# Banded heads among half output tiles, weights ahead of x, gate slabs in the first cross attention, a third MLA weight buffer

## The chip, the cores and the metric

The kernel runs on one core of a Trainium2 chip. The metric is the time of one execution on the device in microseconds; of several runs the median is taken. TensorE multiplies matrices into PSUM, VectorE and ScalarE work element by element and also read PSUM, GpSimd is a slower vector engine, SyncE (SP) mostly starts DMA transfers. Each engine runs its own instructions in order, and engines wait for one another by semaphores.

## What is computed

A model of two blocks over 512 tokens of width 1024, with a memory of 256 tokens, in float32. Cut to what matters:

```
x = x + pool_conv_mixer(rmsnorm(x))              # layer 0; layer 1: x + mla_attention(rmsnorm(x)), 16 heads
x = x + cross_attention(rmsnorm(x), rmsnorm(mem))  # 4 heads of 256; k, v = mem @ wkv; each layer
x = x + conv_ffn(rmsnorm(x))                     # up 1024 -> 2 x 2816, taps, silu, down; each layer
x = rmsnorm(x)                                   # then the second block, one layer:
shift, scale, gate = split(silu(c) @ w_ada + b_ada)
h = rmsnorm(x) * (1 + scale) + shift
sb_q, sb_k, sb_v, sb_g, sw_q, sw_k, sw_v, sw_g = split(h @ w_in)
y_sb = stick_breaking(sb_q, sb_k, sb_v) * silu(sb_g)            # 8 heads of 64
y_sw = window_attention(sw_q, sw_k, sw_v, sinks) * silu(sw_g)   # 8 heads, band of 128 keys and a sink
x = x + gate * (concat(y_sb, y_sw) @ w_out)
return rmsnorm(x)
```

## The kernel before

x lives transposed in SBUF, as 8 tiles of 128 channels by 512 tokens. A weight matrix passes as slabs of 128x2048 elements (1 MB), usually all 1024 input rows by 256 columns. Products are made in three: each slab and each input is split into a high part (ScalarE's copy to fp32r, `w_hi`, `h_hi`) and a low part (VectorE's difference, `w_lo`, `h_lo`), and for each 128x128 piece TensorE does hi*hi, hi*lo and lo*hi. An output tile is 128 channels by 512 tokens, 24 matmuls over 8 pieces, in one PSUM bank; a slab gives two tiles. `ORDER` lists all slabs. `LOADS` is the order in which SP starts their transfers. Split slabs go through two raw buffers and two pairs of `w_hi`, `w_lo`; a slab is split one slab ahead (`split(n + 1)`, on ScalarE and then VectorE), and may overwrite a pair when the slab two before it is done. The slabs of `kv0` (keys and values of the memory, layer 0) and `ada` (`w_ada`, 12 slabs) aren't split; they come into four buffers `whole_buf` that lie on the same memory as the two pairs, and a transfer waits for the slab four before it.

Start: SP starts x in two halves, then the first slab of `pc_in`, rows of parameters, the second slab and mem. TensorE turns x by transposing 128x128 blocks, VectorE copies it (`pre_copy`), ScalarE and VectorE split it (`mix_hi`, `gain_low`). The first tile runs over the first half of the slab, then parameters are turned, then the second tile. The row norms are squares of the transposed tiles, added on VectorE (`mix_add`), summed over channels by a matmul with ones, and rooted (`root`); the norm is applied to the results. mem is treated alike (`mem_add`, `memn_done`) during slabs 1 to 5.

Memory: `memory_0(s)` multiplies the 8 `kv0` slabs, and behind slab s stand `ADA_BEHIND[s]` gate slabs: `ada_row` (16 small matmuls), ScalarE's `ada_copy`, `ada_columns`. VectorE meanwhile makes the convolution (`conv`, 120 taps over all), window sums and the low parts of mem. Then `memory_1` uses the split slabs of `kv1`, whose first two are loaded after the ninth whole slab. Between them come pooled products, the layer norm and `pc_out`.

Cross attention: TensorE does scores of head h, transposes of head h-1's weights, values of head h-1; ScalarE exponentials and scaling, VectorE maxima, copies, low parts. It uses banks 4 to 7.

MLA: heads in pairs; TensorE does scores, values of the pair before, transposes (`turn`), queries two pairs ahead; ScalarE `exponentials` and `scale` into `lp`, two buffers, so that head h's exponentials wait for the transposes of head h-2. Each pair splits one small slab of `uq`, and the fifth pair (heads 12 and 13 ahead) the first full slab of `mla_o`.

Banded heads: after the stick breaking heads, TensorE does per round scores of head h, values of head h-2, transposes of head h-1. VectorE adds the distance and takes the maximum, multiplies values by the gate, copies transposes, takes the reciprocal; ScalarE does exponentials and scaling, and the high parts of outputs. After the last head the four slabs of `w_out` give 8 tiles over all 8 pieces; VectorE adds each to x with the gate and squares it for the last norm, and the result is turned and stored.

The rule that makes TensorE use a slab, in `slab` and `slab_tile` (from line 851 on), is the wait `pe.wait_ge(lo_done, splits_before(n) + 1 + step)`: no matmul of a slab before VectorE has its low part. L835 is the matmul helper, L1441 the activation helper, L1847 the helper of low parts.

## Time and profile before

| what | value |
|---|---|
| median of three runs (1837.98 to 1842.44) | 1841.96 us |
| profiled execution, span of its instructions | 1836.99 us, 1835.3 us |
| busy TensorE, VectorE, ScalarE, GpSimd | 96%, 57%, 37%, 4% |
| mean granted TensorE clock | 0.983 of 2.4 GHz |
| data moved | 164.22 MB |
| head stage of the banded heads | 1719.8 to 1779.8 |
| output projection behind it | 1779.8 to 1823.5 |

A row of the trace's timeline has the start, the duration, the engine, the line of the kernel, the operation, what it writes and reads, and how many were merged into it; in brackets stands how long the engine was idle before it and what it waited for. Matmuls overlap: a duration of 0.39 us for 512 columns goes with starts 0.227 us apart. PEld is TensorE's loading of weights.

### The profile page before, as it was taken

What the parts mean: (1) busy time and instruction counts of PE and PEld (TensorE: products, weight loads), DVE (VectorE), ACT (ScalarE), POOL (GpSimd) and SP (SyncE); (2) the same over time, 40 slices, a digit from 0 to 9 for tenths busy, and PEclk for the clock granted to TensorE, in tenths of its full rate; (3) what the DMA queues carried; (4) which work ended last, traced back from release to release, by engine and by line L of the source; (5) the groups of instructions that cost most, each with busy time, mean ns of one, the idle gap of its engine ahead of it and who ended that gap; (6) DMA issues with size and microseconds to landing.
All of it is one profiled execution on the core that took longest, in us unless ns stands there. A gap on an engine that the chain in (4) does not pass through costs nothing.

```text
span 1835.3 us, 21735 instructions
## 1 busy us (share of the span) xinstructions
PE 1759.1 (96%) x8379; PEld 1402.6 (76%) x8379; DVE 1045.5 (57%) x1416; ACT 686.0 (37%) x1060; POOL 81.9 (4%) x86
## 2 busy tenths in 40 slices
PE   7999999999999999988989999999999999999888
PEld 6877878688888888865557868888888878877667
DVE  6897754465555533566764545655554355344574
ACT  5313443443333322225653343433332122345352
POOL 1000000000000000014540000000000000000000
PEclk9999999999999999999999999999999999999889
DMA  5296442022222332210013202233223222221001
GB/s 185 82 295 207 138 138 92 23 92 92 91 91 91 108 101 89 85 42 15 26 40 115 92 24 92 92 101 104 91 91 103 86 86 92 69 75 47 23 21 50
DMA packets 156695, 164.22 MB, mean 89 GB/s; under 512 B 2934, under 2 KB 153903, under 8 KB 156367
## 3 DMA queue, kind: packets, MB, share of 16 engines
q1 hardware_dynamic: 156000, 162.51, 27.5%
q8 instruction: 49, 0.80, 0.2%
q0 software_dynamic: 240, 0.53, 0.2%
q10 hardware_dynamic: 383, 0.19, 0.0%
q14 instruction: 23, 0.19, 0.0%
HBM read 159.81 MB, written 3.15 MB: 89 GB/s over the span
## 4 chain that ended last, share of the span: by engine, by line
PE 89%; DVE 4%; ACT 3%; issue 1%; DMA 1%; POOL 0%; SPq 0%; DVEq 0%; ACTq 0%
PE bank L835 88%; ACT mla_p L1441 1%; DMA w_raw<-in_pc_w_in_dram 1%; DMA w_whole<-in_xa_wkv_dram 1%; PE bank L1194 1%; ACT w_hi L1441 1%; DVE w_lo L1847 0%; ACT sw_p L1441 0%; ACT h_hi L1441 0%; PE bank L1413 0%; DVE sq L2287 0%; DVE mla_q L2284 0%; DVE xa_pT L2104 0%; DVE nmax L2460 0%; DVE sw_p L2457 0%
## 5 line engine op out<-in xcount | busy, mean ns | idle before, releaser
L835 PE MATMUL bank<-h_hi,w_hi 128*128 128x512 f32 (+1 forms) x1528 | 596.3, 390 | 13.8 <-DVE h_lo L1889 5.4
L835 PE MATMUL bank<-h_hi,w_lo 128*128 128x512 f32 (+1 forms) x1528 | 589.6, 386 | 0.0
L835 PE MATMUL bank<-h_lo,w_hi 128*128 128x512 f32 (+1 forms) x1528 | 589.4, 386 | 0.0
L1847 DVE TENSOR_TENSOR w_lo<-w_raw,w_hi 128x2048 fp32r<-128x2048 f32 (+3 forms) x137 | 294.5, 2149 | 297.4 <-ACT w_hi L1441 297.0
L1441 ACT ACTIVATE w_hi<-w_raw 128x2048 fp32r<-128x2048 f32 (+3 forms) x137 | 245.8, 1794 | 406.4 <-PE bank L835 397.0
L835 PEld LDWEIGHTS bank<-h_hi,w_hi 128*128 128x128 f32 x1528 | 287.9, 188 | 79.2 <-DVE w_lo L1847 10.5
L835 PEld LDWEIGHTS bank<-h_lo,w_hi 128*128 128x128 f32 x1528 | 287.9, 188 | 59.8 <-issue 2.6
L835 PEld LDWEIGHTS bank<-h_hi,w_lo 128*128 128x128 f32 x1528 | 287.7, 188 | 58.0
L835 PE MATMUL bank<-g_hi,w_lo 128*128 128x512 f32 x352 | 136.9, 389 | 0.0
L835 PE MATMUL bank<-g_lo,w_hi 128*128 128x512 f32 x352 | 136.9, 389 | 0.0
L835 PE MATMUL bank<-g_hi,w_hi 128*128 128x512 f32 x352 | 136.9, 389 | 0.0
L1441 ACT ACTIVATE fb<-sq,prm 128x512 f32<-128x512 f32 x44 | 35.9, 816 | 164.9 <-DVE sq L2126 164.9
L2126 DVE TENSOR_TENSOR sq<-bank,rstd 128x512 f32<-128x512 f32 x44 | 30.3, 688 | 94.7 <-PE bank L835 94.6
L1968 DVE SCALAR_TENSOR_TENSOR cv<-glu,prm,cv 128x512 f32<-128x512 f32 x120 | 80.9, 745 | 0.0
L835 PEld LDWEIGHTS bank<-g_hi,w_hi 128*128 128x128 f32 x352 | 66.1, 188 | 13.8
L835 PEld LDWEIGHTS bank<-g_lo,w_hi 128*128 128x128 f32 x352 | 66.1, 188 | 13.8
L835 PEld LDWEIGHTS bank<-g_hi,w_lo 128*128 128x128 f32 x352 | 66.1, 188 | 13.5
L1441 ACT ACTIVATE g_hi<-fb 128x512 f32 (+1 forms) x44 | 27.8, 632 | 105.1 <-DVE fb L2141 105.1
L835 PE MATMUL bank<-mla_k,mla_q 96*128 96x512 f32 (+3 forms) x128 | 47.5, 494 | 14.5 <-ACT mla_p L1441 9.3
L2072 DVE TENSOR_TENSOR x<-x,bank 128x512 f32<-128x512 f32 x32 | 21.9, 685 | 52.5 <-PE bank L835 52.5
L835 PE MATMUL bank<-w_hi,h_hi 128*128 128x256 f32 (+1 forms) x160 | 45.9, 287 | 0.0
L835 PE MATMUL bank<-w_lo,h_hi 128*128 128x256 f32 (+1 forms) x160 | 45.0, 281 | 0.0
(329 smaller groups left out, 2107.2 us busy)
## 6 DMA issues: line engine op xcount, KB each, us to landing
w_raw<-in_ffn_w_up_dram SPq DMA_DIRECT2D x44, 1024.0 KB, 5.1
w_raw<-in_ffn_w_down_dram SPq DMA_DIRECT2D x16, 1024.0 KB, 5.1
w_raw<-in_w_in_dram SPq DMA_DIRECT2D x13, 1024.0 KB, 5.2
w_whole<-in_w_ada_dram SPq DMA_DIRECT2D x12, 1024.0 KB, 7.4
w_whole<-in_xa_wkv_dram SPq DMA_DIRECT2D x8, 1024.0 KB, 7.8
w_raw<-in_xa_wkv_dram SPq DMA_DIRECT2D x8, 1024.0 KB, 6.0
w_raw<-in_xa_wq_dram SPq DMA_DIRECT2D x8, 1024.0 KB, 5.1
w_raw<-in_xa_wo_dram SPq DMA_DIRECT2D x8, 1024.0 KB, 5.1
```

The source lines that it names most:

```text
L835: return nc.tensor.matmul(o, w, v, start=start, stop=stop, **kw)
L1194: m = nc.tensor.transpose(o[:, (i - j) * P:(i - j + 1) * P], lp[:, h % 2, c0:c0 + P], ident[:, :])
L1441: return nc.scalar.activation(o, i, f, **kw)
L1847: return tt(lo_, v, hi.bitcast(f32), SUB)
L1968: m = stt(o, src, w, o, MUL, ADD)
L2072: tt(x[:, i, :], x[:, i, :], bank[(TILE0[stage] + i) % 4][:, :], ADD).then_inc(tile_free, 1)
L2126: tt(sq[j][:, :], bank[(tile + j) % 4][:, :], rstd[:, :], MUL).then_inc(tile_free, 1)
```

## The change

- The first slab's transfer stands ahead of x, and x comes in four quarters. The slab is split before x's tiles are copied. TensorE does both tiles of the first slab piece by piece (two pieces of output per piece of x), with the last four turns of x between.
- Row statistics: ScalarE squares the untransposed rows with a running sum; roots and reciprocals are of 4 columns; the diagonal matrices and a matmul with ones (`spread_root`, between the first and second tile of slab 1) spread them over the partitions, and ScalarE copies the result. mem's rows are scaled before they are turned; the turns of mem come after slabs 2 and 3.
- Gate slabs: one behind each `kv0` slab (8); the other 4 between the transposes and the values of each head of the first cross attention, in banks 0 to 3. The first two slabs of `wo0` are loaded ahead of them, and the first is split at head 2. The gate part of `mod` is made at the first tile of `wo0`.
- MLA: three buffers `lp`; the first `mla_o` slab is split in halves behind pairs 4 and 5.
- Banded heads: `w_out` as four slabs of 512 rows by 512 columns, and 16 half tiles of 12 matmuls. The first eight (upper rows, the stick breaking heads) stand one behind each head's scores; the others follow, three of them cut at the last piece. `w_out`'s second and third slab are split in quarters, one at each head's end. Values of two heads share bank 3; gate and split of them are per pair. VectorE adds 16 half tiles instead of 8 tiles, the first eight among the heads. The high and low parts of the stick breaking outputs are pulled ahead of the heads.

```diff
-ADA_BEHIND = (1, 1, 2, 1, 2, 1, 2, 2)
+ADA_BEHIND = (1, 1, 1, 1, 1, 1, 1, 1)
+ADA_FIRST = sum(ADA_BEHIND)
...
+        if (_name, _s) == ("wq0", 3):
+            ORDER += [("ada", _u) for _u in range(ADA_FIRST, COUNT["ada"])]
...
+LOADS = [_n for _n in LOADS if _n not in (AT["wo0", 0], AT["wo0", 1])]
+LOADS[LOADS.index(WHOLE_SLABS[ROUND]):LOADS.index(WHOLE_SLABS[ROUND])] = [AT["wo0", 0], AT["wo0", 1]]
...
+            for k in range(DT):                      # TensorE, first slab
+                pe.wait_ge(split_lo, SPLIT0["mix0"] + k + 1)
+                for j in range(2):
+                    o, c = bank[j][:, :], slice(j * P, (j + 1) * P)
+                    mm(o, wh[:, k, c], h_hi[:, k, :], k == 0, False)
...
+                if 4 + k < DT:
+                    turn_x(4 + k)
...
+            def spread_root():
+                pe.wait_ge(pre_done, 4 + DT)
+                for b in range(NB):
+                    pe.wait_ge(diag_ready, b + 1)
+                    m = mm(stat[:, b * P:(b + 1) * P], ones[:, :], fb[1][:, b * P:(b + 1) * P], True, True)
+                m.then_inc(mix_step, 1)
...
+            split(FIRST["pc_in"] + 1)                # ScalarE
+            mix_squares(1, range(NB))
             for s in range(6):
                 n = FIRST["pc_in"] + s
-                split(n + 1)
+                if s:
+                    split(n + 1)
                 if s == 0:
...
+                    act.wait_ge(mix_step, 3)
+                    a(rstd[:, :], stat[:, :], ACT.Copy).then_inc(mix_step, 1)
...
+                        if layer == 0:               # TensorE, cross attention
+                            ada_row(ADA_FIRST + g)
                         for d in range(2):
                             o = place("O", g, d)
...
+                        if layer == 0 and g:
+                            ada_columns(ADA_FIRST + g - 1)
...
-                if h >= 2:                           # ScalarE, MLA
-                    act.wait_ge(lt_ready, 3 * (h - 1))
+                if h >= 3:
+                    act.wait_ge(lt_ready, 3 * (h - 2))
...
-                    if pair + 3 <= MH // 2:
+                    if pair + 3 < MH // 2:
                         split(FIRST["uq"] + pair + 3)
                     exponentials(2 * pair + 3)
                     scale(2 * pair + 3)
+                    if pair in OUTPUT_HALF:
...
+                        a(w_hi[k % 2][:, c], raw[k % 2][:, c], ACT.Copy)\
+                            .then_inc(hi_done if pair == max(OUTPUT_HALF) else half_hi, 1)
...
+            for h in range(SWH):                     # TensorE, banded heads
+                window_scores(h)
+                if h >= 2:
+                    window_values(h - 2)
+                out_part(h, 0, 4, so_lo if h == 0 else None)
+                if h:
+                    window_turn(h - 1)
+            window_turn(SWH - 1)
+            out_part(8, 0, 3, wo_lo)
+            window_values(SWH - 2)
+            out_part(9, 0, 3, None)
+            window_values(SWH - 1)
+            out_part(10, 0, 3, None)
+            for u in (8, 9, 10):
+                out_part(u, 3, 4, wo_lo if u == 8 else None)
+            for u in range(11, 16):
+                out_part(u, 0, 4, None)
...
                     act.wait_ge(wrinv_ready, h + 1)  # ScalarE, end of head h
                     for q in range(NB):
                         v = wp[:, h % 2, q, P if q == 0 else 0:]
                         a(v, v, ACT.Copy, scale=rinv[:, h % 2, q:q + 1]).then_inc(wp_ready, 1)
+                    n, c = FIRST["w_out"] + 1 + h // 4, quarter(h)
+                    k = splits_before(n)
+                    act.wait_ge(raw_loaded[k % 2], 16 * (k // 2 + 1))
+                    act.wait_ge(slab_half, 2 * (SPLIT_SLABS[k - 2] + 1))
+                    a(w_hi[k % 2][:, c], raw[k % 2][:, c], ACT.Copy).then_inc(part_hi if h % 4 < 3 else hi_done, 1)
...
+                if 1 <= h <= SWH:                    # VectorE, after the maximum of head h
+                    add_out(h - 1)
...
+                if h < SWH:                          # VectorE, end of head h
+                    n, c = FIRST["w_out"] + 1 + h // 4, quarter(h)
+                    k = pair_of(n)
+                    if h % 4 < 3:
+                        dve.wait_ge(part_hi, 3 * (h // 4) + h % 4 + 1)
+                    else:
+                        dve.wait_ge(hi_done, splits_before(n) + 1)
+                    m = low(w_lo[k][:, c], raw[k][:, c], w_hi[k][:, c])
```

## Rows read from the trace of the kernel before

**Rows 1.** The page, part 1: busy us, share of the span, instructions.
```profile
PE 1759.1 (96%) x8379; PEld 1402.6 (76%) x8379; DVE 1045.5 (57%) x1416; ACT 686.0 (37%) x1060; POOL 81.9 (4%) x86
```
**Rows 2.** Stretches: length, busy us of each engine, granted clock, DMA share, GB/s.
```profile
1719.84:1779.80 59.96, 45.05 (x233) 35.72 (x233) 46.70 (x102) 35.91 (x115) 0.00 (x0) 0.77 0.00 1
...
1725.40:1739.00 13.60, 9.12 (x34) 7.46 (x35) 8.22 (x21) 9.71 (x34) 0.00 (x0) 0.50 0.00 0
...
1759.50:1773.20 13.70, 12.84 (x50) 10.66 (x50) 11.00 (x25) 8.98 (x31) 0.00 (x0) 0.50 0.00 0
...
1779.78:1823.50 43.72, 43.72 (x193) 35.95 (x192) 22.51 (x25) 11.01 (x11) 0.00 (x0) 1.00 0.07 25
```
**Rows 3.** TensorE's waits from 1690 us on: total, times, longest.
```profile
PE bank L1413 <- ACT sw_p L1441: 7.6, 4, 5.9
```
**Rows 4.** Timeline of TensorE in the banded heads.
```profile
1729.88 1.73 PE L1413 MATMUL bank<-ident,sw_p 128*128 128x128 f32 x7 [5.91 <-ACT sw_p L1441]
...
1753.32 1.71 PE L835 MATMUL bank<-sw_pT,sw_v 128*64 128x128 f32 x14 [0.63 <-DVE sw_pT L2480]
1755.79 0.95 PE L1413 MATMUL bank<-ident,sw_p 128*128 128x128 f32 x7 [0.76 <-ACT sw_p L1441]
```
**Rows 5.** Timeline of VectorE in one banded head, and the next head's first row.
```profile
1748.13 1.28 DVE L2457 SCALAR_TENSOR_TENSOR sw_p<-relm,bank 128x128 f32<-128x128 f32 x4
...
1752.04 1.14 DVE L2480 COPY sw_pT<-bank 128x512 f32<-128x512 f32 x2
...
1753.35 0.18 DVE L2485 RECIPROCAL rinv<-rsum 128x4 f32<-128x4 f32 x1
...
1754.80 1.26 DVE L2457 SCALAR_TENSOR_TENSOR sw_p<-relm,bank 128x128 f32<-128x128 f32 x4
```
**Rows 6.** Timeline of ScalarE in the same head.
```profile
1750.96 0.40 ACT L1441 ACTIVATE sw_p<-sw_p,nmax 128x128 f32<-128x128 f32 x1 [1.97 <-DVE nmax L2462]
...
1753.55 0.61 ACT L1441 ACTIVATE h_hi<-fb 64x512 fp32r<-64x512 f32 x1
1754.07 1.58 ACT L1441 ACTIVATE sw_p<-sw_p,rinv 128x128 f32<-128x128 f32 x4
```
**Rows 7.** Timeline of VectorE at the last tile of the output projection.
```profile
1823.70 0.75 DVE L2500 SCALAR_TENSOR_TENSOR x<-bank,mod,x 128x512 f32<-128x512 f32 x1 [3.24 <-PE bank L835]
...
1825.21 0.69 DVE L2507 TENSOR_TENSOR sq<-sq,sq 128x512 f32<-128x512 f32 x1
```
**Rows 8.** The start: TensorE's first big matmuls of slabs 0 and 1; landing of slabs.
```profile
18.15 0.77 PE L835 MATMUL bank<-h_hi,w_hi 128*128 128x512 f32 x1 [5.42 <-DVE h_lo L1889]
...
32.50 0.50 PE L835 MATMUL bank<-h_hi,w_hi 128*128 128x512 f32 x1
```
```profile
DMA to landing us min/median/max: 5.0/5.1/13.1
```
**Rows 9.** Timelines of ScalarE and VectorE ahead of the third input slab.
```profile
34.77 1.28 ACT L1441 ACT_TABLE_LOAD   x1
```
```profile
40.44 2.29 DVE L1847 TENSOR_TENSOR w_lo<-w_raw,w_hi 128x2048 fp32r<-128x2048 f32 x1 [2.50 <-ACT w_hi L1441]
```
**Rows 10.** Timelines of TensorE and VectorE in the stage of the memory.
```profile
128.40 8.64 PE L835 MATMUL bank<-w_whole,m 128*128 128x256 f32 x32 [2.64 <-DMA w_whole<-in_xa_wkv_dram]
136.97 1.07 PE L835 MATMUL bank<-w_whole,c_pad 128*32 128x256 f32 x16
...
138.51 1.07 PE L835 MATMUL bank<-w_whole,c_pad 128*32 128x256 f32 x16
```
```profile
170.59 2.29 DVE L1847 TENSOR_TENSOR w_lo<-w_raw,w_hi 128x2048 fp32r<-128x2048 f32 x1 [8.94 <-ACT w_hi L1441]
```
```profile
172.94 0.38 PE L835 MATMUL bank<-h_hi,w_hi 128*128 128x256 f32 x1 [2.03 <-DVE w_lo L1847]
```
**Rows 11.** TensorE's waits in the first cross attention, 318 to 357 us.
```profile
PE bank L835 <- DVE xa_pT L2104: 2.9, 4, 1.2
```
**Rows 12.** MLA, the fifth pair: ScalarE, VectorE, TensorE, and the stretch behind.
```profile
943.99 1.90 ACT L1441 ACTIVATE w_hi<-w_raw 128x2048 fp32r<-128x2048 f32 x1
```
```profile
945.92 2.29 DVE L1847 TENSOR_TENSOR w_lo<-w_raw,w_hi 128x2048 fp32r<-128x2048 f32 x1 [3.79 <-ACT w_hi L1441]
```
```profile
949.83 1.29 PE L835 MATMUL bank<-mla_k,mla_q 96*128 96x512 f32 x2 [3.68 <-ACT mla_p L1441]
```
```profile
950.60:957.40 6.80, 6.80 (x20) 2.99 (x20) 3.90 (x10) 2.37 (x6) 3.78 (x3) 0.50 0.00 0
```

454 lines of the change are left out of this document (251 added, 203 removed).

## The prediction

> **What bounds the kernel now.** The first view to read is the page's share of busy time: TensorE 96%, VectorE 57%, ScalarE 37% [rows 1]. TensorE sets the pace almost everywhere, so the other engines matter only where TensorE waits for them. The second view is the table of stretches with the granted clock [rows 2]: the stage of the eight banded heads takes 59.96 us, TensorE is busy in 45.05 of them, and its clock is 0.77 on average, that is 1.2 GHz in 13.6 us around 1732 and again in a stretch like it at 1759 to 1773. The output projection behind it takes 43.72 us for 193 matmuls, 0.227 us each, with TensorE never idle. The list of waits says what the heads wait for: the weights of ScalarE, 7.6 us in four times [rows 3]. Last come the timelines around every other wait of TensorE: the start, the memory keys and values, the first cross attention, the end of MLA. All that the change can gain lies in those places; the feed-forward stages, some 900 us with no wait, it does not touch.
>
> **Part 1, the heads among half output tiles.** Before, the projection starts when all heads are done: 60.0 + 43.7 = 103.7 us. The change puts eight half tiles (12 matmuls, 2.72 us each) behind the heads' scores, so TensorE has per head: scores about 2.0, values 1.7 (the next score or transpose follows at once), transposes 0.95 [rows 4], output 2.7, together 7.3 us. If that were the pace, 8 x 7.3 plus what remains would be the time. It isn't, because VectorE and ScalarE get a longer circle. Before, one head on VectorE runs from 1748.13 to the next head's 1754.80: masks and maximum take until ScalarE begins its exponentials at 1750.96, the sum's reciprocal is there at 1753.53, and VectorE goes on to the next head while ScalarE still scales [rows 5, 6]; 6.67 us per head. After the change VectorE ends each head with the low part of a quarter slab, and waits for that on ScalarE's high part, which stands behind the four scalings of the same head. So the circle closes through all of it: 2.83 (to the exponentials) + 2.2 (exponentials and the sink) + 0.4 (sum, reciprocal) + 1.6 (scaling [rows 6]) + 0.6 (quarter, high: the 128x512 copy of rows 6) + 0.7 (quarter, low: a 128x512 subtraction costs as the 0.69 of rows 7) = 8.3 us. In odd heads VectorE has the new update of x (0.75 [rows 7]), the gate of a pair (0.7) and the copies (1.16 [rows 5]) before the reciprocal and is 0.3 late: 8.6. Queued behind the waiting VectorE are the next head's masks; queued behind those, ScalarE's exponentials and then TensorE's transposes. In head 4 TensorE also waits for the second output slab, whose last quarter comes only at the end of head 3; it has then some 4 us of slack until VectorE wants its transposes, and uses them.
>
> The head chain starts 0.7 us later than the 1722.48 of before (three low parts of the first heads are pulled ahead of the last gate, one stands ahead of the masks): 1723.2. Eight circles, 8.3 (four early or even ones and head 1, which has no pair yet: five) and 8.6 (three): 67.3, to 1790.5. The third output slab is complete there; behind it come eight half tiles, 21.8 us, and two value steps of 1.65: 1815.5, where before ended at 1823.5. VectorE has to add eight tiles from 1800.5 at 2.2 us each (0.75 + 0.69 + 0.69 and gaps [rows 7]): 1817.7 instead of 1825.9. The tail behind it (transposes, root, store) is the same. **Gain 8.2 us**; of this I take off 1.0 for a clock dip: after the first head TensorE waits some 3 us for a copy, and in this trace the waits of 2.64, 3.68 and 5.91 us [rows 10, 12, 4] were each followed by a fall of the clock to 1.2 GHz. The heads have slack for most of it. Bounds: at the pace of TensorE alone 7.3 us per head, gain 17; at 9.5 us per head (TensorE at half clock needs 13 us for a head, so one dip of 13.6 us may add 5), gain 0.
>
> **Part 2, the start.** Before, the first big matmul runs at 18.15, after the first slab, sent behind x, has landed (13.1 us from issue [rows 8]) and been split; the second slab's matmuls begin at 32.50 [rows 8]. After: the first slab lands at about 6, its halves are split by 11, and then VectorE makes one copy and one low part of x per step (1.45 us), the first at 13.1. TensorE has 48 matmuls and four turns of x; the first 4 to 5 us at 1.2 GHz, as from 18.15 on before, then 2.4 GHz: done at about 28.2, parameters turned at 28.8, so 3.7 us earlier. But the statistics now return through TensorE behind the third tile (34.2), then ScalarE copies, VectorE evicts two tiles, ScalarE loads the sigmoid's table (1.28 [rows 9]) and only then splits the third slab: its low part ends at 42.1, where before had 42.7 (40.44 + 2.29 [rows 9]) with 0.7 to spare; now TensorE is there at 40.2 and waits 1.9. The removed squares, sums and 512-wide reciprocals were beside other work. 3.7 - 1.9 = **gain 1.7 us** (rounded from 1.8; the turns of mem are only moved). Bounds -1 (clock rises late, x in four pieces lands late) to 4 (no wait).
> The trace's table loads take 1.28 us each. The Trainium skill, ScalarE: Activation LUTs, Table sets: the hidden batching unit, puts one load at about 2.7 us and advises to batch by set; the change adds a square root of its own for mem. By that figure the wait above would be 3.3 and this part's gain 0.3 (an estimate from that page). This case's rows disagree, and I go by them.
>
> **Part 3, keys, values and gate slabs.** From the end of the input projection (89.50) to the first split slab of the second layer's memory (172.94) pass 83.4 us. Four of twelve gate slabs leave this stage: 4 x 1.54 (136.97 to 138.51) = 6.2 us; with 16 slabs instead of 20 the transfers keep up, so the wait of 2.64 and the dip behind it (8.64 instead of 7.15 for a slab) go: 4.1. Together 10.3. What is late next is VectorE: it works without a gap from 89.5 to 161.65 (it idles 8.94 before 170.59 [rows 10]) on the convolution, then makes the low part, 2.29: 72.15 + 2.3 = 74.45 us after the stage's start. So 83.4 - 74.45 = 9.0, and TensorE now waits 3.6 instead of 2.03 there, which I price with 2.0 for a clock dip (3.4 us at half speed up to 6.8). The moved slabs cost 6.2 us in the cross attention, less the 2.9 us of four waits that they fill [rows 11]: 3.3. The split of the first output slab that goes with them stands in front of ScalarE's and VectorE's parts of head 1's output (1.9 + 2.3 us); TensorE has 3.6 us of values and 3.6 of scores meanwhile, so it costs nothing, and 2 us if that cover fails. SP passes two loads ahead of the four gate slabs; each has 11 us. 9.0 - 2.0 - 3.3 = **gain 3.7 us**; bounds 0 to 7.
>
> **Part 4, MLA.** Every pair of heads takes 15.07 us with one wait of 0.9. The chain there runs from TensorE's query over VectorE's query, shuffle and reciprocal, ScalarE's scaling, the small split, the maxima and the exponentials back to the scores. A third buffer lets exponentials start 0.6 us earlier in a place that is not on that chain: 0. The gain is in the fifth pair: there the full split of the output slab (1.90 + 2.29) makes TensorE wait 3.68, and the clock falls for 6.8 us, worth 3.4 [rows 12]. Halves of 0.95 + 1.15 go behind pairs 4 and 5 instead. There they hold VectorE, which waits for ScalarE's scaling (1.92) first, so the next pair's maxima come some 4 us late, and its query and rotary step on GpSimd with them. Following that through: the next scores start at 948.8 (before 949.83), at full clock, and the output projection at 967.9 instead of 971.8. 3.9, less 0.9 for the chance of another dip: **gain 3.0 us**; bounds -2 (the halves delay both pairs and the clock falls anyway) to 6.
>
> **Sum.** 7.2 + 1.7 + 3.7 + 3.0 = 15.6 us. The profiled execution took 1836.99 us, 1835.3 of span and 1.7 around it, and would become 1821.4. The median of the three timed runs, 1841.96, is 5.0 above it; the time that I forecast is of such a median: 1841.96 - 15.6 = 1826.4.
>
> **The rivals.** (a) The heads run at TensorE's pace: ScalarE and VectorE find the quarters' time beside their waits, the period is 7.3 instead of 8.45, 9 us more: 1817. For it: TensorE is idle in a third of a head before. Against it: the order of the quarter behind the scaling on two engines. In sentences that the rest does without: the Trainium skill, TensorE: Matmul & The Clock Gate, What's actually happening, says that throttled is the default and activity releases it; by that, more matmuls among the heads keep 2.4 GHz and favour this case. (b) The circle is as said but a dip or the extra reads of PSUM stretch it to 9.5: the projection's hidden half is paid back, and only the other parts' 8.4 remain: 1834. (c) Slower than before: TensorE stays at 1.2 GHz in half of the head stage, as it did in 27 of 60 us. A head at half clock needs 13.4 us of TensorE (twice scores, values, transposes and half tile, less what overlaps), a mean of 10.9, 20 us more than forecast: 1846. It decides above 10.4 us per head. Against it: the 5.9 us of waiting that stood ahead of the first low stretch [rows 4] are gone, and full work brought the clock back each time. (d) The change doesn't do what it says outside the heads: gate slabs find no gaps, MLA's halves cost what the split did, the start is held by the third slab: 1834.5 with the heads' gain alone.
>
> **How the numbers follow.** Forecast 0.50, (a) 0.15, (b) 0.17, (c) 0.09, (d) 0.09. The likeliest is 1826.4. The range takes in (a)'s upper and (b)'s and (d)'s bulk: 1814 to 1837; what is left out is (c) and the far ends. A measurement of this kernel can tell about 0.3%, 5.5 us: faster means below 1836.4. Forecast, (a), most of (b) and (d): 0.83; within: 0.08; slower: 0.09.
>
> **What would show it.** In the profile after: VectorE's next masks starting right behind the quarter's low part, 8.3 to 8.6 us per head, and ScalarE's quarter right behind the scaling (if the period is near 7.3, (a)). The stretch from the end of the values of the last old head to the end of the projection about 96 us. A wait of about 2 us ahead of the third input slab, at 40. A wait of 3 to 4 us ahead of the first split slab of the memory, and VectorE without idle time before it. Four filled waits in the first cross attention. No wait of 3.7 in MLA, two smaller ones. The forecast is wrong if the clock's low stretches grow in number, or if VectorE's end of the convolution isn't what the memory stage waits for.

## The result and the profile after

The changed kernel took 1821.70 us, the median of five runs (1818.93 to 1822.52), beside 1838.88 us for the kernel before on the same chip (five runs, 1837.98 to 1842.44). The ratio is 0.9904, with a 95% interval of 0.9892 to 0.9917: faster by 0.96%, or 17 to 18 us. The profiled execution took 1821.70 us, with a span of 1819.9 us, 15.4 less than before.

The page of the changed kernel, part 1, against [rows 1]: TensorE is busy 6 us less, the span is 15.4 us shorter.

```profile
PE 1753.1 (96%) x8383; PEld 1397.9 (77%) x8383; DVE 1032.3 (57%) x1407; ACT 687.1 (38%) x1072; POOL 82.0 (5%) x86
```

To find where the time went, the same instruction of each stage is read in the timeline of TensorE in both kernels. First the kernel before: the start of the memory's keys, of the first cross attention, of the MLA keys, of the second cross attention, of the spreading of the last inner norm, of the last stick breaking values, of the final transposes.

```profile
90.33 1.97 PE L835 MATMUL bank<-m,w_whole 128*128 128x256 f32 x8 [0.83 <-issue]
321.68 1.13 PE L835 MATMUL bank<-xa_kT,xa_qT 128*128 128x256 f32 x4 [0.79 <-DVE xa_qT L2089]
795.89 0.41 PE L835 MATMUL bank<-ckv_hi,w_hi 128*64 128x512 f32 x1 [1.53 <-DVE ckv_lo L1889]
1063.31 0.92 PE L835 MATMUL bank<-memn,xa_qT 128*128 128x256 f32 x3 [0.78 <-DVE xa_qT L2089]
1505.96 0.71 PE L835 MATMUL bank<-fb,ones 128*128 128x128 f32 x4 [1.22 <-DVE fb L2343]
1717.46 0.64 PE L835 MATMUL bank<-sb_w,sb_v 128*64 128x512 f32 x1
1824.50 0.77 PE L1427 MATMUL bank<-ident,y 128*128 128x128 f32 x5 [0.91 <-DVE x L2500]
```

The same places in the changed kernel:

```profile
90.16 2.18 PE L863 MATMUL bank<-m,w_whole 128*128 128x256 f32 x9 [0.83 <-issue]
313.97 0.70 PE L863 MATMUL bank<-xa_kT,xa_qT 128*128 128x256 f32 x2 [0.78 <-DVE xa_qT L2189]
790.96 0.42 PE L863 MATMUL bank<-ckv_hi,w_hi 128*64 128x512 f32 x1 [1.53 <-DVE ckv_lo L1992]
1054.83 0.48 PE L863 MATMUL bank<-memn,xa_qT 128*128 128x256 f32 x1 [0.78 <-DVE xa_qT L2189]
1497.52 0.80 PE L863 MATMUL bank<-fb,ones 128*128 128x128 f32 x2 [1.22 <-DVE fb L2460]
1709.97 0.64 PE L863 MATMUL bank<-sb_w,sb_v 128*64 128x512 f32 x1
1809.11 1.09 PE L1498 MATMUL bank<-ident,y 128*128 128x128 f32 x8 [0.91 <-DVE x L2583]
```

Differences of differences give each part of the gain:

| part | forecast | measured in the two profiles |
|---|---|---|
| start and input projection | 1.7 | 0.17 |
| keys, values, layer norm, `pc_out` | 9.0 less 2.0 | 7.54 |
| first cross attention (gate slabs in it) up to MLA | -3.3 | -2.78 |
| MLA | 3.0 | 3.55 |
| second cross attention and feed forward | 0 | -0.04 |
| from the last inner norm to the last stick breaking values | 0 | -0.95 |
| banded heads and output projection | 8.2 less 1.0 | 7.90 |
| sum | 15.6 | 15.39 |

The sum is right to 0.2 us, in part by luck: the start gave 1.5 less than forecast and the stage ahead of the heads lost 0.95, and each of the other four rows with a term gave 0.5 to 0.7 more than it. Single rows of this table also hold the chance of the clock in two profiles, up to 1.9 us in one place, as the experiments show.

**The heads.** One head of the changed kernel on VectorE: masks, maximum, the update of x, the copies, the reciprocal, then 2.19 us of idling for ScalarE's quarter, and the next head's masks right behind the quarter's low part.

```profile
1737.16 0.18 DVE L2617 RECIPROCAL rinv<-rsum 128x4 f32<-128x4 f32 x1
1739.53 0.69 DVE L1950 TENSOR_TENSOR w_lo<-w_raw,w_hi 128x512 fp32r<-128x512 f32 x1 [2.19 <-ACT w_hi L1512]
1740.14 1.28 DVE L2593 SCALAR_TENSOR_TENSOR sw_p<-relm,bank 128x128 f32<-128x128 f32 x4
```

ScalarE in the same stretch: exponentials, scaling, the quarter's high part, and then 3.47 us of idling for the next head's maximum.

```profile
1734.78 0.40 ACT L1512 ACTIVATE sw_p<-sw_p,nmax 128x128 f32<-128x128 f32 x1 [3.47 <-DVE nmax L2598]
...
1737.38 1.60 ACT L1512 ACTIVATE sw_p<-sw_p,rinv 128x128 f32<-128x128 f32 x4 [0.44 <-DVE rinv L2617]
1738.88 0.61 ACT L1512 ACTIVATE w_hi<-w_raw 128x512 fp32r<-128x512 f32 x1
1742.96 0.40 ACT L1512 ACTIVATE sw_p<-sw_p,nmax 128x128 f32<-128x128 f32 x1 [3.47 <-DVE nmax L2598]
```

From one head's exponentials to the next head's, 1734.78 to 1742.96, pass 8.18 us, 6.67 before [rows 5]. The circle closes as 2.60 (exponentials to scaling) + 1.50 (scaling) + 0.65 (quarter, high) + 0.61 (quarter, low) + 2.82 (masks and maximum, 1740.14 to 1742.96) = 8.18, and it is the same in all seven periods. Both engines idle in it, each for the other: two engines that are 57% and 38% busy set the pace.

**The start.** TensorE at the third input slab, then an instruction six further on, 0.63 us long, as are its neighbours, which start 0.43 us apart instead of 0.23:

```profile
40.90 0.50 PE L863 MATMUL bank<-h_hi,w_hi 128*128 128x512 f32 x1 [1.83 <-DVE w_lo L1950]
...
42.70 0.63 PE L863 MATMUL bank<-h_hi,w_hi 128*128 128x512 f32 x1
```

The granted clock of the stretch around it (length, busy us by engine, clock, DMA share, GB/s):

```profile
41.40:45.40 4.00, 4.00 (x12) 3.08 (x12) 2.75 (x5) 3.76 (x5) 0.00 (x0) 0.58 0.81 262
```

ScalarE waited 3.49 us for the spread root and VectorE 4.52 us for ScalarE's copy of it (the first row), and only behind that came the third slab's split (the last row is its high part):

```profile
33.65 0.60 ACT L1512 ACTIVATE rstd<-bank 128x512 f32<-128x512 f32 x1 [3.49 <-PE bank L863]
34.26 1.28 ACT L1512 ACT_TABLE_LOAD   x1
...
36.62 1.90 ACT L1512 ACTIVATE w_hi<-w_raw 128x2048 fp32r<-128x2048 f32 x1
```

### The profile page after: what moved, and what is told of

Its sections match the earlier page's. It is cut to its first block, busy times and chain, and to the rows that moved or that the text cites. A ratio compares the mean times of both kernels' runs of the same rounds, so it can differ in the third digit from the quotient of the medians.

```text
span 1819.9 us, 21744 instructions
## 1 busy us (share of the span) xinstructions
PE 1753.1 (96%) x8383; PEld 1397.9 (77%) x8383; DVE 1032.3 (57%) x1407; ACT 687.1 (38%) x1072; POOL 82.0 (5%) x86
## 4 chain that ended last, share of the span: by engine, by line
PE 82%; DVE 11%; ACT 4%; issue 1%; POOL 1%; DMA 1%; SPq 0%; DVEq 0%; ACTq 0%
PE bank L863 81%; DVE cv L2061 3%; ACT sw_p L1512 1%; DVE w_lo L1950 1%; ACT mla_p L1512 1%; ACT w_hi L1512 1%; DVE sw_p L2593 1%; DVE nmax L2596 1%; DMA x_nat<-in_x_dram 1%; PE bank L1240 0%; ACT mla_p_b L1512 0%; ACT h_hi L1512 0%; DVE nmax L2400 0%; DVE sq L2394 0%; DVE x L2583 0%
## 5 line engine op out<-in xcount | busy, mean ns | idle before, releaser
L1950 DVE TENSOR_TENSOR w_lo<-w_raw,w_hi 128x2048 fp32r<-128x2048 f32 (+4 forms) x144 | 297.0, 2063 | 309.8 <-ACT w_hi L1512 309.4
L1512 ACT ACTIVATE w_hi<-w_raw 128x2048 fp32r<-128x2048 f32 (+4 forms) x144 | 246.8, 1715 | 380.8 <-PE bank L863 374.9
L863 PE MATMUL bank<-w_hi,h_lo 128*128 128x256 f32 (+1 forms) x160 | 45.0, 281 | 0.0
```

The costliest lines, as they stand in the source:

```text
L863: return nc.tensor.matmul(o, w, v, start=start, stop=stop, **kw)
L1512: return nc.scalar.activation(o, i, f, **kw)
L1950: return tt(lo_, v, hi.bitcast(f32), SUB)
```

## The experiments

All times are medians of four to eleven runs, and compared with the kernel before, run on the same chip; the ratio stands with each. The changed kernel's own ratio is 0.9904 (0.9892 to 0.9917).

**The circle of the heads (1).** Only ScalarE's order changes: the quarter's high part ahead of the wait for the reciprocal.

```diff
                     a(esink[:, h % 2, :], nmax[:, h % 2, :], ACT.Exp, ...).then_inc(wexp_done, 1)
+                    a(w_hi[k % 2][:, c], raw[k % 2][:, c], ACT.Copy).then_inc(part_hi if h % 4 < 3 else hi_done, 1)
...
                     act.wait_ge(wrinv_ready, h + 1)
...
-                    a(w_hi[k % 2][:, c], raw[k % 2][:, c], ACT.Copy).then_inc(part_hi if h % 4 < 3 else hi_done, 1)
```

> The changed kernel, with ScalarE's high part of each quarter slab moved from behind the four scalings to ahead of the wait for the reciprocal (right behind the head's exponentials). Nothing is added or left out. Theory (the head's circle runs masks 2.8, exponentials 2.2, reciprocal 0.4, scaling 1.6, quarter high 0.6, quarter low 0.7, in all 8.2): the scaling drops out of the circle, which becomes 6.2 plus the 0.6 of the high part at most, so TensorE's own 7.3 us per head set the pace. Period of the heads 7.3 to 7.5 instead of 8.19, the gap of 5.3 us ahead of the last transposes smaller, 8 x 0.8 = 6.4 us less: about 1815. Rival: the period is set elsewhere (banks of PSUM, TensorE's order, the copies), stays at 8.2, and the time is that of the changed kernel, 1821.7.

Measured: 1812.66 us, ratio 0.9849 (0.9834 to 0.9864). The timeline of VectorE, where the quarter's low part now follows the reciprocal without a wait:

```profile
1728.20 0.18 DVE L2617 RECIPROCAL rinv<-rsum 128x4 f32<-128x4 f32 x1
1728.52 0.69 DVE L1950 TENSOR_TENSOR w_lo<-w_raw,w_hi 128x512 fp32r<-128x512 f32 x1
1729.13 1.27 DVE L2593 SCALAR_TENSOR_TENSOR sw_p<-relm,bank 128x128 f32<-128x128 f32 x4
```

And ScalarE's exponentials of two heads in a row, 6.14 us apart:

```profile
1725.81 0.40 ACT L1512 ACTIVATE sw_p<-sw_p,nmax 128x128 f32<-128x128 f32 x1 [1.95 <-DVE nmax L2598]
...
1731.95 0.40 ACT L1512 ACTIVATE sw_p<-sw_p,nmax 128x128 f32<-128x128 f32 x1 [1.94 <-DVE nmax L2598]
```

The circle did set the pace. The later periods, with values and pairs in them, are 6.4 to 7.7, and the mean of all seven is 6.62 us. So 9.0 us were gained where 6.4 were expected: I had counted 7.3 us of TensorE's work for every head, while the first two rounds have no values. Over eight rounds scores, half tiles, transposes and values are 8 x 1.71 + 8 x 2.94 + 7 x 0.95 + 6 x 1.65 = 53.8, or 6.7 each. TensorE is the bound now: in this stretch it is busy 60.86 of 65.70 us, where before it was 45.05 of 59.96 [rows 2].

```profile
1714.40:1780.10 65.70, 60.86 (x331) 48.26 (x330) 49.60 (x108) 38.01 (x117) 0.00 (x0) 0.97 0.05 17
```

**Half tiles behind the heads (2).** TensorE's eight half tiles and VectorE's updates leave the heads.

```diff
                 window_scores(h)
                 if h >= 2:
                     window_values(h - 2)
-                out_part(h, 0, 4, so_lo if h == 0 else None)
...
+            for u in range(16):
+                out_part(u, 0, 4, {0: so_lo, 8: wo_lo}.get(u))
```

> The changed kernel with its first eight half output tiles moved from among the heads to behind them (VectorE's eight updates of x too). The quarters of the second output slab stay at the ends of heads 0 to 3; the third slab can then only be split after the first is used, so heads 4 to 7 have no quarter. Theory (the half tiles fill TensorE's idle time and are not on the circle, the quarters are): heads 0 to 3 keep a period of 8.2 us, heads 4 to 7 fall back to 6.7, and the eight half tiles, 21.8 us, stand behind: 21.8 - 4 x 1.5 = 15.8 more, about 1837. Rival: TensorE's half tiles set the period, so that all heads run at 6.7 without them: 21.8 - 8 x 1.5 = 9.8 more, 1831.5.

Measured: 1836.47 us, ratio 0.9983 (0.9973 to 0.9993). ScalarE's exponentials of heads 3 to 6:

```profile
1743.18 0.40 ACT L1506 ACTIVATE sw_p<-sw_p,nmax 128x128 f32<-128x128 f32 x1 [3.47 <-DVE nmax L2593]
...
1751.37 0.40 ACT L1506 ACTIVATE sw_p<-sw_p,nmax 128x128 f32<-128x128 f32 x1 [3.46 <-DVE nmax L2593]
...
1756.66 0.40 ACT L1506 ACTIVATE sw_p<-sw_p,nmax 128x128 f32<-128x128 f32 x1 [1.10 <-DVE nmax L2593]
...
1762.81 0.40 ACT L1506 ACTIVATE sw_p<-sw_p,nmax 128x128 f32<-128x128 f32 x1 [1.95 <-DVE nmax L2593]
```

With a quarter 8.19 us, without one 5.3 and 6.15 in turn (the kernel before had 6.67; gate and split are now per pair). The half tiles don't lengthen the circle by anything; a quarter costs 2 to 3 us per head, though its two instructions are 1.3 us long. So the theory of this run was right on the half tiles and too high on the heads without a quarter (6.7 expected). The time is 14.8 us above the changed kernel's: 21.8 for the eight tiles behind the heads, less some 7.9 for four heads without a quarter (head 7's exponentials begin at 1768.10 instead of 1775.72, and the stage 0.2 later); the rest, 0.9, isn't traced.

**The start (3).** The third slab's split ahead of the two waits for the spread root.

```diff
+                    split(n + 2)                     # ScalarE, s == 0
                     act.wait_ge(mix_step, 3)
...
+                    split(n + 2)                     # VectorE, s == 0
                     dve.wait_ge(mix_step, 4)
```

> The changed kernel, with the split of the third input slab on ScalarE and VectorE moved ahead of their waits for the spread root (ScalarE idles 3.49 us and VectorE 4.52 us there). Theory (the wait of 1.83 us ahead of the third slab comes from that order, and the fall of the clock to half for 3.4 us right behind it comes from the wait): the third slab begins at 39.1 without a wait, the clock doesn't fall, and the input stage ends 1.8 + 1.7 = 3.5 us earlier than 89.3: about 1818. Rival 1: the clock falls at this place whatever TensorE waited, then only 1.8. Rival 2: a later wait takes it back (the last slab's wait of 0.9, or a larger wait for the memory slabs), then 0 to 1.

Measured: 1819.17 us, ratio 0.9890 (0.9873 to 0.9907), 2.5 less, which the intervals alone don't tell from none. The trace does: the wait is gone, the clock is full where it was 0.58, and the memory's keys start at 86.82 instead of 90.16.

```profile
37.70:42.00 4.30, 4.30 (x20) 3.56 (x19) 1.12 (x3) 4.04 (x7) 0.00 (x0) 1.00 0.32 112
```

Of the 3.3 us, 0.9 is given back behind the wait of 3.42 at the first split memory slab, where the clock this time fell for 6.8 us instead of 3.4.

The other profiles part the wait from the fall. Of the changed kernel's first profile and those of the twelve experiments, ten (all but 3, 11 and 12) have the wait of 1.83 us; in eight the clock falls for 3.4 us behind it, in those of experiments 1 and 5 it doesn't. Experiment 1 at the same place, and the stretch behind:

```profile
41.66 0.50 PE L863 MATMUL bank<-h_hi,w_hi 128*128 128x512 f32 x1 [1.83 <-DVE w_lo L1950]
```

```profile
41.66:45.66 4.00, 4.00 (x18) 3.31 (x19) 2.60 (x5) 3.76 (x5) 0.00 (x0) 1.00 0.76 238
```

From the third slab to the memory's keys it is 47.65 us in experiment 1 (89.31 less 41.66) and 49.26 with the fall (90.16 less 40.90): the fall costs 1.6 us and the wait 1.8, and one can come without the other. The same start, in ten profiles, also varies by the clock at its beginning: the first big matmuls are slow until 14.3 to 15.2 us in the eight with the fall and until 16.3 and 16.7 in the two without it. In the present experiment, without the wait, they are slow until 16.3, as in those two, so this profile doesn't show that the fall was kept away by taking out the wait; experiment 12's does better, slow until 14.7, no wait and no fall, but it is one profile.

**VectorE's taps (4).** Eight taps move into VectorE's idle time in the input stage (the list of each slab's count).

```diff
-                conv([0, 0, 4, 9, 6, 4][s])
+                conv([0, 0, 9, 7, 11, 4][s])
...
-                conv(10)
+                conv(9)
```

> The changed kernel, with eight taps of the convolution (0.67 us each on VectorE) moved from the keys and values stage into VectorE's idle time in the input stage: 9, 7, 11, 4 taps in its last four slabs instead of 4, 9, 6, 4, and 9 instead of 10 behind each of the eight memory slabs. Theory (VectorE's gapless work from the stage's start sets when the first split memory slab may begin, with a wait of 3.41 us and a fall of the clock behind it; nine taps in one slab delay the last input slab by 0.9): VectorE reaches that slab 5.4 us earlier, the wait of 3.41 goes, the fall behind it (1.4) too, and 0.9 goes at the last input slab: 5.7 us less, about 1816. Rival 1: a transfer or ScalarE's high part comes next and leaves 1 to 2 us of the wait, with the fall of the clock: 1818 to 1820. Rival 2: VectorE isn't what this stage waits for, then 1821.7 less at most 0.9.

Measured: 1818.06 us, ratio 0.9882 (0.9865 to 0.9899), 3.6 less. The last input slab's wait of 0.9 is gone. At the first split memory slab the wait is 2.05 instead of 3.41; VectorE, free 66.0 us after the stage's start instead of 71.2, idles there for ScalarE's high part, which stands behind ScalarE's copies of the last unsplit slab's results:

```profile
158.60 2.29 DVE L1950 TENSOR_TENSOR w_lo<-w_raw,w_hi 128x2048 fp32r<-128x2048 f32 x1 [3.84 <-ACT w_hi L1512]
...
160.95 0.42 PE L863 MATMUL bank<-h_hi,w_hi 128*128 128x256 f32 x1 [2.05 <-DVE w_lo L1950]
```

So VectorE was the limit, as forecast, and ScalarE's order is the next one: the slab begins only 1.4 us earlier after the stage's start (72.2 instead of 73.6). This is the first rival's case.

**Gate slabs back (5).**

```diff
-ADA_BEHIND = (1, 1, 1, 1, 1, 1, 1, 1)
+ADA_BEHIND = (1, 1, 2, 1, 2, 1, 2, 2)
...
-                        if layer == 0:
-                            ada_row(ADA_FIRST + g)
```

> The changed kernel with all twelve gate slabs back behind the slabs of the memory's keys and values (1, 1, 2, 1, 2, 1, 2, 2 of them), none in the cross attention, and the output slabs loaded in their plain order. Theory: the stage up to the first split memory slab takes 83 us again instead of 73.6 (6.2 of TensorE's own work and 2.6 of a wait for a transfer, and VectorE idles before the slab), and the cross attention gets its four waits back and loses the 6.2 us: 9.0 - 1.4 of a clock fall - 2.8 = 4.8 more, about 1826.5. Rival: the moved slabs were no gain, because VectorE's taps fill the time anyway: less than 1.5 more.

Measured: 1827.91 us, ratio 0.9937 (0.9922 to 0.9952), some 6 more than the changed kernel. The wait for a transfer and the smaller wait at the split slab are back, at the sizes of [rows 10] (2.66, and 2.02 at 170.29):

```profile
126.99 7.17 PE L861 MATMUL bank<-w_whole,m 128*128 128x256 f32 x32 [2.66 <-DMA w_whole<-in_xa_wkv_dram]
```

From the memory's keys (88.91) to the cross attention (319.06) it takes 230.15 us, 6.3 more than the changed kernel, and the cross attention is 2.8 shorter: 3.5 net in this profile. In it the clock didn't fall behind the wait of 2.66, which in [rows 10] it did (8.64 instead of 7.15 us for a slab); of the six executions three took 1825.7 to 1826.3 at a mean clock of 0.988 to 0.989, this one among them, and three 1829.6 to 1831.3 at 0.985 to 0.986. The median lies between them.

**MLA, each edit undone alone (6, 7) and both (8), beside the changed kernel once more (9).**

```diff
-                if h >= 3:                           # 6: two buffers
-                    act.wait_ge(lt_ready, 3 * (h - 2))
+                if h >= 2:
+                    act.wait_ge(lt_ready, 3 * (h - 1))
...
-        OUTPUT_HALF = {4: slice(SLAB // 2, SLAB), 5: slice(0, SLAB // 2)}
+        OUTPUT_HALF = {}                             # 7: full split, at pair + 3 <= MH // 2
```

> The changed kernel with two instead of three buffers of MLA weights (exponentials of head h wait for the transposes of head h-2 again); the halves of the output slab stay behind pairs 4 and 5. Theory (the third buffer lets ScalarE start earlier in a place that isn't on the chain): the pair period stays 15.07 us, the time stays within 0.5 us of 1821.7. Rival: the third buffer is what absorbs the halves, and without it the waits of 1.2 and 1.6 us around the fifth pair become one of 3 or more with a fall of the clock: 2 to 4 us more, 1824 to 1826.

> The changed kernel with the first output slab of MLA split whole in the fifth pair, as before, instead of in halves behind pairs 4 and 5; the three buffers stay. Theory (the full split makes TensorE wait about 3.7 us, and a fall of the clock for 6.8 us comes behind that): the last transposes come 3.5 us later after the stage's start, 1825. In the kernels so far the same stretch with halves showed a fall of 3.4 or 6.8 us in some profiled executions and none in others, worth up to 1.7, so 1823.5 to 1825.5. Rival: the third buffer absorbs the full split, as the wait stands at the exponentials: no wait over 2 us there, 1822.

> The changed kernel with both MLA edits undone: two buffers of weights and the full split in the fifth pair. Theory (halves are worth what the wait of 3.7 costs, and the profile of the changed kernel flattered them, because the clock happened not to fall there): from the scores of the pair ahead of the split to the last transposes 38.6 us, as in the kernel before, against 34.8 to 36.7 with halves; 2 to 3 us more than the changed kernel run beside it. Rival: the MLA edits are worth what the two profiles differ by, 3.6 to 3.8 us more. Second rival: each edit alone cost 1 to 1.5 us within the spread, and both together no more than that.

> The changed kernel itself once more, beside the kernel with the MLA edits undone. It shows how far two profiled executions of the same program differ: the same waits in the same places, but a stretch of half clock behind the last two pairs of MLA in some executions and not in others. 1821.7 within 1.5 us expected; if the MLA stretch from the scores at 927 to the last transposes takes 36.7 instead of 34.8, that stretch's price is the clock's chance and no property of the kernel. Rival: the differences between the experiments' MLA stretches come from the edits elsewhere, and this run repeats 34.8 and the clock's low stretches at the same instructions.

Measured: two buffers 1823.24, ratio 0.9908 (0.9894 to 0.9923); full split 1822.95, 0.9914 (0.9901 to 0.9928); both undone 1823.67, 0.9921 (0.9906 to 0.9936); the changed kernel again 1822.17, 0.9909 (0.9895 to 0.9924). By time no single edit can be told from none: two buffers came out 1.5 us above the changed kernel's median, where 0.5 was expected at most, and the ratios differ by 0.0004. The theory of 7, some 2 to 4 us more, isn't borne out (1.3 by the medians). Both together are worth 1.5 us by the medians and 2.2 by the ratios, at the edge of what is measured.

The same stretch, from the scores ahead of the split to the last transposes, in the first profile of the changed kernel and in its second, and with both edits undone:

```profile
927.32:962.14 34.82, 28.27 (x164) 17.58 (x165) 25.32 (x52) 22.63 (x63) 11.45 (x9) 1.00 0.08 28
```

```profile
927.55:962.63 35.08, 29.91 (x165) 18.18 (x165) 25.56 (x52) 22.51 (x63) 11.42 (x9) 0.95 0.08 28
```

```profile
927.31:965.94 38.63, 31.33 (x165) 18.93 (x165) 24.21 (x51) 22.87 (x62) 11.42 (x9) 0.91 0.07 26
```

The same program ran this stretch at full clock once and with a fall of 3.4 us the next time. In experiment 1, which has the same instructions here, it fell for 6.8 us:

```profile
926.25:962.99 36.74, 31.59 (x164) 18.80 (x165) 25.53 (x52) 22.49 (x63) 11.42 (x9) 0.91 0.08 27
```

So both MLA edits together are worth 38.63 - 36.74 = 1.9 us at an equal clock, and up to 3.8 where the clock happens to stay. Each alone can be read at a fall of 3.4 us, which the second profile of the changed kernel (35.08) shares with experiment 6 (two buffers, halves) and experiment 7 (three buffers, full split), in this order:

```profile
927.12:963.50 36.38, 29.90 (x164) 18.28 (x165) 25.62 (x52) 22.72 (x63) 11.43 (x9) 0.95 0.08 27
```

```profile
926.76:962.38 35.62, 29.63 (x165) 18.40 (x165) 24.03 (x51) 22.53 (x62) 11.43 (x9) 0.95 0.08 28
```

The third buffer gives 36.38 - 35.08 = 1.3 us and the halves 35.62 - 35.08 = 0.5, by one profile of each. The pair's period is 15.07 with two buffers and with three, as forecast. The third buffer works behind a fall of the clock: TensorE's wait at the next to last scores is then 0.22 instead of 0.96, and that at the last transposes 0.89 instead of 1.46. With the full split the wait of 3.67 is there, and the halves have one of 1.22 and one of 1.62 in its place.

Both kernels with the full split, and the kernel before, have a low stretch of 6.8 us at the last inner norm, and all nine profiles with halves and without fillers one of 10.2, with the same waits of 1.22 and 2.47. That is the 0.95 of the table. It goes with the halves and not with the buffers (experiment 6 has 10.2, experiment 7 has 6.8), so by these profiles the halves alone lose there more than the 0.5 that they gain in MLA. Why the stretch is longer with halves isn't settled.

**Useless matmuls in the waits (10).** Written to a bank that nobody reads.

```diff
+            def filler(o, w, v, count):
+                for _ in range(count):
+                    mm(o, w, v, True, True)
...
             mix_pooled((0, 1))
+            filler(bank[5][:, :], pw_hi[:, 0, :], pooled_hi[:, 0, :], 12)
...
+                if s:                                # second slab of the MLA keys
+                    filler(bank[5][:, :], wh[:, 0, 0:P], wh[:, 0, 0:512], 14)
...
+            filler(bank[3][:, :], cq_hi[:, 0, 0:P], cq_hi[:, 0, :], 14)
             scores(0)
...
+            filler(bank[5][:, :], kept[:, 0:P], kept[:, 0:512], 4)
             spread(bank[6], fb[0], NB)
+            filler(bank[5][:, :], kept[:, 0:P], kept[:, 0:512], 9)
```

> The changed kernel with matmuls of no use in four of TensorE's waits, written to a bank that nobody reads: 12 (128x128 by 512 columns, 0.227 us each at full clock) before the first split memory slab (wait 3.41), 14 before the second slab of the MLA keys (wait 3.79), 14 before the first MLA scores (wait 4.12), and 4 and 9 around the spreading of the last norm (waits 1.22 and 2.47). Nothing is left out, no other work moves. Theory (the falls of the clock to half speed behind these places, 3.4, 3.4, 6.8 and 10.2 us long, come from TensorE's idling): they vanish or shrink, and with them 1.4 + 1.6 + 1 to 3 + 2 us: 1815 to 1817. Rival: the falls have another cause and stay; the fillers end inside the waits and the time is 1821.7, or 1 to 4 us more where a filler at half clock outlasts its wait.

Measured: 1820.38 us, ratio 0.9893 (0.9878 to 0.9907). Stretches of the changed kernel first, behind the first split memory slab, the first MLA scores, the last inner norm (length, busy us, clock):

```profile
163.73:171.70 7.97, 7.97 (x51) 7.88 (x52) 3.47 (x3) 0.77 (x2) 0.00 (x0) 0.79 0.82 257
840.54:851.50 10.96, 10.96 (x35) 6.42 (x36) 4.52 (x11) 3.28 (x11) 4.78 (x4) 0.69 0.00 0
...
1497.52:1506.00 8.48, 6.01 (x17) 4.92 (x18) 6.67 (x12) 3.20 (x5) 0.00 (x0) 0.50 0.00 0
```

With fillers, the last inner norm first:

```profile
1495.25:1503.70 8.45, 8.27 (x34) 6.50 (x34) 6.14 (x14) 2.88 (x6) 0.00 (x0) 0.80 0.01 2
163.00:171.00 8.00, 7.82 (x59) 7.55 (x60) 4.00 (x5) 1.84 (x4) 0.00 (x0) 1.00 0.82 249
842.00:853.00 11.00, 9.56 (x42) 5.88 (x42) 5.45 (x13) 5.68 (x16) 8.03 (x7) 1.00 0.00 1
```

In this profile the falls are gone in two places and shorter in the third; by the timelines that gives 1.5, 3.3 and 1.0 us. Only 1.3 are left of them, because the fourth group stood eight tiles behind the wait that it was meant to fill (the 3.79 us ahead of the MLA keys' fifth tile) and cost its own 3.2 us and a longer fall of the clock (6.8 us instead of 3.4). The theory held in three places; the fourth was only tried in experiment 12.

**Together (11), and together with fillers (12).** The edits of experiments 1, 3 and 4, and the first split memory slab's high part ahead of the last unsplit one's copies:

```diff
             for s in range(8):
...
+                if s == 7:
+                    split(AT["kv1", 0])
                 kv_out(0, s)
-            split(AT["kv1", 0])
```

> The changed kernel with three orders changed at once: ScalarE's quarter ahead of the scaling in the banded heads, the third input slab's split ahead of the waits for the spread root, eight taps earlier; and, new, ScalarE's high part of the first split memory slab ahead of its copies of the last unsplit one's results (with the taps moved, VectorE idled 3.84 us for that high part, and 2.05 us of TensorE's wait stayed). Theory: the gains lie in separate places and add up, 9.0 + 2.5 + 3.6, and the last wait of 2.05 with the fall of the clock behind it gives 3 more: 1821.7 - 18.1 = 1803.6, and no wait before that memory slab. Rival: another wait takes its place (the transfer of the slab, or the pooled products), and the sum of the three stays: 1806.6 or a little more.

> The four orders of the kernel with all changes together (1802.2), with useless matmuls in three of TensorE's waits: 14 at the fifth tile of the MLA keys (wait 3.79, where the earlier run had its 14 eight tiles too late, without a wait to cover them), 14 before the first MLA scores (wait 4.12), 4 and 9 around the spreading of the last norm. Theory (the clock falls come from idling, and the covered waits cost nothing): the falls of 6.8 us behind the first two go, that behind the third shrinks to 3.4; gains of 1.7 to 3.3, 3.3 and 1.0: about 1795. Rival: a fall that is kept away in one place comes at the next wait (the clock falls by the sum of the waits and not by the one ahead of it), and less than 2 us is gained: over 1800.

Measured: 1802.19 us, ratio 0.9790 (0.9777 to 0.9802), and 1796.25 us, ratio 0.9766 (0.9753 to 0.9780). In the first no wait is left before the memory slab, and the gains add up to within 1.4 us of the expectation. In the second, the misplaced group stands at the right tile and leaves 0.62 of a wait of 3.79:

```profile
787.99 3.33 PE L863 MATMUL bank<-w_hi 128*128 128x512 f32 x14
791.94 0.44 PE L863 MATMUL bank<-ckv_hi,w_hi 128*64 128x512 f32 x1 [0.62 <-DVE mla_k L2394]
```

TensorE is busy 98% of the span, at a mean clock of 0.997. This version beats both kernels, the changed one by 1.4%.

## Why the prediction was right, and where it wasn't

**Forecast and time.** 1826.4 was forecast for the median by taking 15.6 off a median of 1841.96; the timed difference is 17.2 by the medians of the two kernels beside each other. The kernel before ran at 1838.9 there, and from that 15.6 would have given 1823.3. So of the 4.7 us between forecast and time 3.1 are the base and 1.6 the gain.

**Part 1, the heads.** The circle through both engines held: 8.3 and 8.6 forecast, 8.18 to 8.20 measured in every head. What was missing was that the extra work of odd heads (0.3) fits into VectorE's 2.19 of idling; so three heads were 0.4 shorter than forecast. The first masks came at 1715.55; with the last stick breaking values 7.5 earlier than before, that is 1723.0 on the scale of the forecast, which had 1723.2. The end comes 7.9 earlier, where 8.2 less 1.0 was forecast. (With its own steps of 2.2 the forecast's end, 1800.5 + 8 x 2.2, is 1818.1 and not 1817.7, so its 8.2 should have been 7.8.) The dip of 1.0 came in another form: TensorE didn't wait some 3 us behind the first head (its waits there are 1.06, 0.73 and 0.85), and yet the clock fell there for 6.8 us, from 1724.8, and for 3.4 from 1745.3. The period stayed at 8.19 through both, so the heads' slack covered them whole. TensorE waited 5.34 us for the last head's scaling, and with that came a last fall of 3.4, from 1779.4. At head 4 the second slab's last quarter made no wait in this profile, and one of 1.36 us in four others (experiments 5, 6, 9 and 10), off the circle. By the Trainium skill, TensorE: Matmul & The Clock Gate, What's actually happening, activity releases the throttle; the traces agree: the head stage ran at a mean clock of 0.91 with half tiles in it, and at 0.77 before and in experiment 2 without them.

**Part 2, the start.** This step failed. Forecast 3.7 - 1.9 = 1.7, measured 0.17, and by the nine profiles with this same start, whose memory stage begins at 88.9 to 90.5 us, from nothing to 1.4 against the one profile before. The first slab went better than forecast (the second slab's matmuls begin at 26.96 against 32.50 of [rows 8]; the forecast was 28.8; the first big matmuls, from 12.88 on, were slow for 1.9 us and not for the 4 to 5 that were forecast), and the wait came as forecast, 1.83 against 1.9. But of the 5.5 us at the second slab 5.4 are gone by the memory stage: 1.83 for that wait; 1.6 for the fall of the clock behind it, which I left out although parts 1, 3 and 4 each priced one (it came in eight of ten profiles with that wait); 0.9 for the last slab's wait, because VectorE's copies of mem's turns now stand ahead of nine taps and of that slab's low part (from 65.75 us, when VectorE has waited 4.39 for these turns, it works without a gap to that low part; experiment 4: the wait went with two taps fewer there); and 0.8 for the spreading, which stands behind the third tile where the sums of the norm stood ahead of it before. That makes 5.1; the last 0.3 isn't traced. "The turns of mem are only moved" was the wrong sentence: a moved step delays what is queued behind it in its new place. The tables were loaded in 1.28 us again, as the rows of before had it, and the next instruction began 0.01 us later. The Trainium skill, ScalarE: Activation LUTs, Table sets: the hidden batching unit, has 2.7 us for one; the measurement decides, and the wait of 1.83 instead of 3.3 agrees with it.

**Part 3, keys, values and gate slabs.** Forecast 74.45 us from the stage's start to the first split slab, measured 73.57 (163.73 less 90.16), and 3.6 of waiting, measured 3.41. The limiter was named rightly: VectorE without a gap, shown by experiment 4. The dip cost 1.5 instead of 2.0, the moved slabs 2.8 instead of 3.3. The whole part gave 4.8 in the profiles, 3.7 forecast; experiment 5 puts it at 3.5 to 6.

**Part 4, MLA.** 3.55 in the profiles against 3.0. The experiments show that this agreement is the clock's: at an equal clock the two edits together give 1.9, and 0.95 is given back at the last inner norm. By time the part is worth 1.5 to 2.2. Two terms were wrong in size. The halves were to give 3.9 less 0.9, the wait at the full split and the fall behind it; but behind a fall of 3.4 us the halves alone save 0.5, since their own waits of 1.22 and 1.62 take the place of most of the 3.67, and the clock falls behind them too in some executions. The third buffer was put at 0 because the pair's period doesn't hang on it; that is right of the period, but behind a fall it gives 1.3.

**The rivals.** (a), heads at TensorE's pace, didn't happen, and experiment 1 shows that one moved instruction makes it happen, for 9.0 us, the size that (a) had. (b) is refused: the period was 8.19 and not 9.5. (c) is refused: the clock was better in the heads, not worse. (d) is refused for part 3, partly true of part 4 and nearly true of the start.

**What is open.** Why the low stretch at the last inner norm is longer in all kernels with halves; and why the clock falls behind the same wait in one execution and not in another. The start as a whole was not undone in any run, so its gain is known from the profiles alone.

## What to carry to other kernels

When work is added to two engines that hand a tile back and forth, write down the circle instruction by instruction and ask for each added one whether it has to stand in it: here 0.6 us of ScalarE behind a scaling made another engine wait 2.19, and moving it ahead of a wait that was there anyway gave 9 us. Look for order before work: the three single experiments that gained most (1, 4 and 3) only put instructions elsewhere in the queue of their own engine and add nothing. A single profile of a stretch with falls of the clock can flatter an edit by the edit's own size; compare the stretch in several profiles, or at equal clock. Here, at an equal fall, the credit in MLA went from the halves to the third buffer.

## What the runs showed of the hardware

TensorE's clock fell to 1.2 GHz behind a wait of only 1.83 us, in eight of ten profiles, for 3.4 us each time, at a price of 1.6; the waits that the prediction had priced were 2.64 and more. It also fell without a wait of that length. In the heads of the changed kernel it fell at 1724.8, behind waits of 1.06 and 0.73 us with transposes and scores of 128 columns between. At the last inner norm it fell at 1496.1, ahead of the waits of 1.22 and 2.47 us, while TensorE was doing small matmuls, 16 of 1 column and from 1495.23 on 8 of 2 columns:

```profile
1493.53 1.84 PE L863 MATMUL bank<-ones,sq 128*128 128x1 f32 x16
```

Useless matmuls in the waits kept the clock at 2.4 GHz and cost nothing where they ended inside the wait: 14 of them at the first MLA scores gave 3.3 us, and in the last kernel the mean clock rose from 0.991 to 0.997. Put where there is no wait they cost their full time and brought no better clock. This too is activity releasing the throttle, as the section of the Trainium skill named above says. And the same program had a fall of 3.4 us in MLA in its second profile, at a place where it had none in its first.
